# Another order for the second attention stage of a three-stage transformer kernel

## The reference

```python
def compress_blocks(a, pe, w1, w2):          # keys or values in overlapping blocks of 32
    ...
    blocks = blocks + pe[:, None, :]
    return jax.nn.gelu(flat @ w1) @ w2

def nsa_attend(q, gates, k_cmp, v_cmp, k_slc, v_slc, k_win, v_win):
    ...
    p_c = masked_softmax(s, ...)             # over the compressed blocks
    p_s = masked_softmax(s, dist_s >= 0)     # over the selected blocks: here all, as there are four
    p_w = masked_softmax(s, mask_w)          # over the window: here all earlier tokens
    return gi[..., 0:1] * o_c + gi[..., 1:2] * o_s + gi[..., 2:3] * o_w

def nsa_layer_mix(h, shared, mem_k, mem_v, w_in, w_out):
    q, gl, mq = split_cols(h @ w_in, [NSA_WIDTH, 3 * NSA_HEADS, MEM_WIDTH])
    gates = jax.nn.sigmoid(gl.reshape(B, T, NSA_HEADS, 3))
    o = nsa_attend(q * NSA_DH ** -0.5, gates, *shared)
    m = mem_attend(mq, mem_k, mem_v)         # four heads over 256 memory tokens
    return jnp.concatenate([o, m], axis=-1) @ w_out
```

## Time and profile before

| | |
|---|---|
| time of the runs shown | 1009.38 us, the median of 3 (1009.30 to 1010.58) |
| time of the profiled execution | 1014.77 us |
| its span, first to last instruction | 1013.5 us |
| mean granted clock of PE | 0.978 of 2.4 GHz |
| PE matmul, PE weight load | busy 968.8 and 940.7 us |
| DVE, ACT, POOL | busy 662.7, 504.5 and 25.3 us |

### The profile page before, as it was taken

The page is one execution under the profiler, slowest core; times in us unless marked ns, Lnnn a source line. Parts: engine busy times, 40 slices in busy tenths (PEclk is TensorE's granted clock), DMA queues, the critical chain, the costliest instruction groups (busy, mean ns, idle before and its releaser), DMA issues.

```text
span 1013.5 us, 18812 instructions
## 1 busy us (share of the span) xinstructions
PE 968.8 (96%) x7963; PEld 940.7 (93%) x7963; DVE 662.7 (65%) x1196; ACT 504.5 (50%) x837; POOL 25.3 (2%) x29
## 2 busy tenths in 40 slices
PE   6899999999999999887899999999999899999998
PEld 5899989999999998776899999999988799999998
DVE  5778856786767676664488676767455386556564
ACT  5544545554545473764456454546234364444442
POOL 0000000000000000000000000000022000000000
PEclk9999999999999989989999999999999899999999
DMA  9433333455454534331254645454321145454541
GB/s 353 164 146 125 125 125 114 178 196 219 152 219 152 222 137 136 125 126 42 74 218 177 229 167 208 167 209 156 136 92 63 55 161 213 168 207 167 208 167 42
DMA packets 24851, 160.66 MB, mean 159 GB/s; under 512 B 2880, under 2 KB 4672, under 8 KB 6080
## 3 DMA queue, kind: packets, MB, share of 16 engines
q1 hardware_dynamic: 24192, 159.20, 42.5%
q10 hardware_dynamic: 576, 0.26, 0.1%
HBM read 158.14 MB, written 1.05 MB: 157 GB/s over the span
## 4 chain that ended last, share of the span: by engine, by line
PE 87%; DVE 8%; ACT 3%; issue 1%; DMA 1%; SPq 0%; DVEq 0%; ACTq 0%
PE ps L358 86%; DVE wl L1134 3%; PE ps L367 1%; ACT wh L1889 1%; DMA raw<-in_w 1%; ACT arena L2121 1%; DVE arena L1566 1%; DVE xl L1143 0%; DVE col L1143 0%; DVE arena L1391 0%; DVE arena L1615 0%; DVE arena L1198 0%; SPq L2321 0%; DVE arena L1190 0%; DVE arena L1379 0%
## 5 line engine op out<-in xcount | busy, mean ns | idle before, releaser
L1134 DVE TENSOR_TENSOR wl<-raw,wh 128x1024 fp32r<-128x1024 f32 x292 | 342.0, 1220 | 156.3 <-ACT wh L1889 156.3
L358 PE MATMUL ps<-xh,wh 128*128 128x256 f32 (+1 forms) x1312 | 374.2, 285 | 10.7 <-DVE wl L1134 9.7
L358 PE MATMUL ps<-xl,wh 128*128 128x256 f32 (+1 forms) x1312 | 369.3, 282 | 0.0
L358 PE MATMUL ps<-xh,wl 128*128 128x256 f32 (+1 forms) x1312 | 368.9, 281 | 0.0
L1889 ACT CAST wh<-raw 128x1024 fp32r<-128x1024 f32 x292 | 290.2, 1046 | 155.9 <-PE ps L358 144.4
L358 PEld LDWEIGHTS ps<-xh,wh 128*128 128x128 f32 x1312 | 249.3, 190 | 14.2 <-DVE wl L1134 9.9
L358 PEld LDWEIGHTS ps<-xh,wl 128*128 128x128 f32 x1312 | 249.3, 190 | 0.0
L358 PEld LDWEIGHTS ps<-xl,wh 128*128 128x128 f32 x1312 | 249.3, 190 | 0.0
L358 PE MATMUL ps<-fh,wh 128*128 128x256 f32 x528 | 148.6, 282 | 0.0
L358 PE MATMUL ps<-fl,wh 128*128 128x256 f32 x528 | 148.6, 281 | 0.0
L358 PE MATMUL ps<-fh,wl 128*128 128x256 f32 x528 | 148.4, 281 | 0.0
(11 more groups left out here) (212 smaller groups left out, 1060.0 us busy)
## 6 DMA issues: line engine op xcount, KB each, us to landing
raw<-in_w SPq DMA_DIRECT2D x145, 1024.0 KB, 4.8
raw<-in_w SPq DMA_DIRECT2D x2, 512.0 KB, 6.0
arena<-in_mem SPq DMA_DIRECT2D x1, 1024.0 KB, 12.2
out<-xt SPq DMA_DIRECT2D x8, 128.0 KB, 2.0
small<-in_small SPq DMA_DIRECT2D x1, 943.5 KB, 9.0
arena<-in_sel SPq DMA_DIRECT2D x3, 256.0 KB, 5.5
xt<-in_x SPq DMA_DIRECT2D x2, 256.0 KB, 4.3
xt<-in_x SPq DMA_DIRECT2D x1, 512.0 KB, 6.3
```

The source lines that it names most:

```text
L358: return pe.matmul(out, lhsT, rhs, start=start, stop=stop, skip_group_check=True)
L1134: v.tensor_tensor(L[:, s], src[:, s], f32(H[:, s]), ALU.subtract).then_inc(*w_lo.up(2 * i + a))
```

## The change

The program computes the same, with these differences:

- Bq0 stands third in the list of units, in front of kvv; ck1 stands in front of Bq1.
- The squares of the tokens for stage B are taken at the end of f0, between the entries of chunks, and DVE adds them up to two (`square_sums("B")`), so that PE's sums are the short form that the other stages use (`sums`), placed between the halves of kvk. In all residuals the squares are taken later, and DVE's sums stand together at the start of the feed-forward stage.
- kvv comes after the gates are turned. The first score work of a pair, the compression halves, the halves of Bq1, Bm0 and Bm1 and the turns follow each other in another order; memory heads 0 and 1 run beside pairs 2 and 3.
- The gates' sigmoid is written as 1 / (1 + exp(−x)): ACT exponentiates, DVE adds 1 and takes the reciprocal.
- The four small transfers of the compression blocks go from ACT's queue to SP's, in front of the load of Bq1.
- Bo0, Bo1 and Bo2 are each ended before the next is (chunks 4 to 7 of each in one piece), and Co0 to Co2 of the last attention stage are ended in turn.
- Banks and the engines' lists follow.

```diff
-        + ["kvc", "kvk", "kvv", "Bq0", "ck0", "Bq1", "ck1", "cv0", "cv1", "Bm0", "Bm1",
+        + ["kvc", "kvk", "Bq0", "kvv", "ck0", "ck1", "Bq1", "cv0", "cv1", "Bm0", "Bm1",
...
         unit_f("kvc", 0, CH, CL, kv_in)
-        P = ps.open("sums_B", 4)
-        t.wait_ge(*ps.vacant("sums_B"))
-        for c in range(8):
-            t.wait_ge(*s_sq.at(SQ["B"] + c))
-            for n in range(2):
-                last = mm(P[:, n:n + 1], sqB[c][:, n * 128:(n + 1) * 128], cn("inv", 0, 1), c == 0 and n == 0, c == 7)
-        last.then_inc(*ps.full("sums_B"))
-        unit_f("kvk", 1, CH, CL, kv_in)
+        part_f("kvk", 1, range(0, 4), kv_in, CH, CL)
+        sums("B", 4)
+        part_f("kvk", 1, range(4, 8), kv_in, CH, CL)
         norm_spread("B", 5, rst_)
-        unit_t("kvv", lambda: 2, CH, CL, kv_in)
         unit_f("Bq0", 3, XH, XL, x_b)
         P = ps.open("gates", 0)
...
         nsa_scores(0)
-        squeeze(0, 0, 1)
-        P = ps.open("gates_t", 2)
+        P = ps.open("gates_t", 1)
         t.wait_ge(*ps.vacant("gates_t"))
         t.wait_ge(*ps.done("gates"))
...
-        part_f("Bq1", 0, range(0, 4), x_b)
+        unit_t("kvv", lambda: 2, CH, CL, kv_in)
         nsa_scores(1)
-        part_f("Bq1", 0, range(4, 8), x_b)
+        squeeze(0, 0, 0)
+        nsa_turn(0)
         squeeze(0, 1)
-        nsa_turn(0)
+        part_f("Bq1", 1, range(0, 4), x_b)
+        nsa_out(0)
+        nsa_turn(1)
+        part_f("Bq1", 1, range(4, 8), x_b)
+        nsa_out(1)
         squeeze(1, 0, 2)
-        nsa_out(0)
+        nsa_scores(2)
         squeeze(1, 1)
-        nsa_turn(1)
-        part_f("Bm0", 0, range(0, 4), x_b)
-        P = ps.open("gT", 1)
+        nsa_scores(3)
+        part_f("Bm0", 1, range(0, 4), x_b)
+        P = ps.open("gT", 0)
...
-        nsa_out(1)
-        nsa_scores(2)
-        part_f("Bm0", 0, range(4, 8), x_b)
+        nsa_turn(2)
         P = ps.open("kvm", 2)
...
-        nsa_scores(3)
+        part_f("Bm0", 1, range(4, 8), x_b)
+        blocks_scores(0, (7, 0))
+        blocks_scores(1, None)
+        nsa_out(2)
+        mem_scores(1, 0, 4, mqB, qB)
         part_f("Bm1", 1, range(0, 4), x_b)
-        blocks_scores(2, 0)
-        nsa_turn(2)
+        nsa_turn(3)
+        mem_scores(1, 1, 0, mqB, qB)
+        blocks_turn(7)
         part_f("Bm1", 1, range(4, 8), x_b)
-        mem_scores(1, 0, 0, mqB, qB)
-        nsa_out(2)
-        blocks_turn(7)
-        nsa_turn(3)
-        mem_scores(1, 1, 1, mqB, qB)
-        mem_turn(1, 0, 0)
+        mem_turn(1, 0, 4)
         nsa_out(3)
         blocks_out()
+        mem_out(1, 0, 5)
         mem_scores(1, 2, 7, mqB, qB)
-        mem_out(1, 0, 1)
-        mem_turn(1, 1, 0)
-        out_part("Bo0", lambda: 4, (0, 1), out_b, 0, 7)
-        mem_scores(1, 3, 7, mqB, qB)
-        out_part("Bo1", lambda: 5, (0, 1), out_b, 0, 7)
...
+        mem_turn(1, 1, 4)
+        mem_scores(1, 3, 0, mqB, qB)
+        out_part("Bo0", lambda: 6, (0, 1), out_b, 0, 7)
+        mem_out(1, 1, 7)
+        mem_turn(1, 2, 4)
+        out_part("Bo1", lambda: 1, (0, 1), out_b, 0, 7)
+        mem_out(1, 2, 5)
+        mem_turn(1, 3, 4)
         out_part("Bo0", None, (2, 3), out_b, 0, 7)
-        mem_out(1, 3, 1)
         out_part("Bo1", None, (2, 3), out_b, 0, 7)
+        mem_out(1, 3, 7)
+        out_part("Bo2", lambda: 2, (0, 1), out_b, 0, 7)
         out_part("Bo2", None, (2, 3), out_b, 0, 7)
         for j in range(3):
-            out_part(f"Bo{j}", None, (4, 5), out_b, 0, 7)
-        for j in range(3):
-            out_part(f"Bo{j}", None, (6, 7), out_b, 0, 7)
-        out_part("Bo3", lambda: 7, KORD, out_b, 0, 7)
+            out_part(f"Bo{j}", None, range(4, 8), out_b, 0, 7)
+        out_part("Bo3", lambda: 3, KORD, out_b, 0, 7)
```

VectorE's list, cut to the first half of the stage:

```diff
+        square_sums("B")
         rests("kvc", 2)
         token_variance("B")
...
         queries(0)
+        rests("Bq0", 2)
         d.wait_ge(*d_even.at(3))
...
-        rests("Bq0", 2)
+        d.wait_ge(*ps.ready("gates"))
+        v.tensor_copy(gz, ps["gates"][0:24, 0:T]).then_inc(*ps.freed("gates"))
+        nsa_scores(0)
+        d.wait_ge(*ps.done("gates_t"))
+        v.tensor_scalar(gt, gt, 1.0, None, ALU.add).then_inc(*n_ge.up(1))
+        d.wait_ge(*n_ge.at(1))
+        v.reciprocal(gt, gt).then_inc(*n_ge.up(2))
...
+        rests("kvv", 2)
+        nsa_probs(0)
+        nsa_scores(1)
...
         rests("ck0", 2)
-        nsa_probs(0)
+        nsa_probs(1)
+        rests("ck1", 2)
         rests("Bq1", 2)
-        nsa_scores(1)
         queries(1)
-        rests("ck1", 2)
-        nsa_probs(1)
         rests("cv0", 2)
+        nsa_scores(2)
+        nsa_probs(2)
+        nsa_scores(3)
+        take("gT", gT, 120)
         rests("cv1", 2)
...
+        add_up("Bo0", 0, "f1")
         rests("Bo0", 3)
-        add_up("Bo0", 0, "f1")
+        split_two(0, "f1", "gffn1")
+        residual("Bo1", 1, "f1", "gffn1")
         rests("Bo1", 3)
```

ScalarE's list, and the transfers on SyncE's:

```diff
+            for c in ((), (0, 1), (2, 3), (4, 5, 6, 7))[q]:
+                squares("B", c, xs[c])
...
-        a.wait_ge(*n_evn.at(0))
-        for g in range(2):
-            for par in range(2):
-                s.dma_start(X25[par * 64:(par + 1) * 64, :, g, :], ev5[g * 64:(g + 1) * 64, :, par, :]).then_inc(
-                    *d_even.up(2 * g + par))
...
+        for n in range(2):
+            last = s.activation(gt[:, n * 24:n * 24 + 24], ps["gates_t"][:, n * 24:n * 24 + 24], ACT.Exp,
+                                scale=nrst[:, 1 - n:2 - n])
+        last.then_inc(*ps.freed("gates_t"))
         nsa_exps(0)
...
         casts("ck0", 2)
+        nsa_exps(1)
+        nsa_turned(0)
+        casts("ck1", 2)
         casts("Bq1", 2)
...
+        nsa_turned(1)
+        casts("cv0", 2)
+        nsa_exps(2)
         gelu(0)
...
+            if NAMES[i] == "Bq1":
+                q.wait_ge(*n_evn.at(0))
+                for g in range(2):
+                    for par in range(2):
+                        load(X25[par * 64:(par + 1) * 64, :, g, :], ev5[g * 64:(g + 1) * 64, :, par, :], d_even, 2 * g + par)
```

The last attention stage, on PE:

```diff
-        for j in range(3):
-            out_part(f"Co{j}", None, (0, 1), out_c)
-        for j in range(3):
-            out_part(f"Co{j}", None, (2, 3), out_c)
+        out_part("Co0", None, (0, 1), out_c)
+        out_part("Co1", None, (0, 1), out_c)
+        out_part("Co0", None, (2, 3), out_c)
+        out_part("Co2", None, (0, 1), out_c)
+        out_part("Co1", None, (2, 3), out_c)
+        out_part("Co2", None, (2, 3), out_c)
```

More of the change, by code:

```diff
@@ L778, in nsa_out, with blocks_scores @@
             last.then_inc(*n_pv.up(j))
-        def blocks_scores(*on):
-            for g in range(2):
-                ps.open(f"cs{g}", on[g])
-                t.wait_ge(*ps.vacant(f"cs{g}"))
+        def blocks_scores(n, on):
+            if n == 0:
+                for g in range(2):
+                    ps.open(f"cs{g}", on[g])
+                    t.wait_ge(*ps.vacant(f"cs{g}"))
             t.wait_ge(*ps.done("kvm"))
             t.wait_ge(*ps.done("Bq1"))
-            for n in range(2):
[L788 to L794, removed]
+            for j in range(4):
+                for g in range(2):
+                    r = g * 64
+                    last = mm(ps[f"cs{g}"][:, n * 64 + j * 16:n * 64 + j * 16 + 15],
+                              bq[r:r + 64, j, (1 - n) * 128:(2 - n) * 128], kcm[r:r + 64, 0:15], True, True)
+                    if n == 1 and j == 3:
+                        last.then_inc(*ps.full(f"cs{g}"))
         def blocks_turn(bank):
@@ L813, in blocks_out, with part_f @@
                     last.then_inc(*ps.full(name))
-        def part_f(name, bank, chunks, ready):
+        def part_f(name, bank, chunks, ready, a_h=XH, a_l=XL):
             i = U[name]
@@ L1518, in dve_program @@
         by_rs("kvk", kk, rs_[:, 0:T])
[L1519 to L1524, removed]
+        v.tensor_scalar(nrst, rst_[:, 0:2], -1.0, None, ALU.mult).then_inc(*n_ge.up(0))
         def queries(n):
@@ L1622, in dve_program @@
                             ALU.subtract).then_inc(*n_rl.up(kv))
-        d.wait_ge(*ps.ready("gates"))
-        v.tensor_copy(gz, ps["gates"][0:24, 0:T]).then_inc(*ps.freed("gates"))
-        nsa_scores(0)
-        g0 = gt[:, 24:48].rearrange("p (h n) -> p h n", n=3)[:, :, 0]
-        d.wait_ge(*ps.done("gates_t"))
-        v.tensor_scalar(g0, g0, cn("valid", 0, 1), None, ALU.mult).then_inc(*n_gt.up(0))
+        rests("kvv", 2)
+        nsa_probs(0)
+        nsa_scores(1)
+        d.wait_ge(*ps.ready("kvv.0"))
+        for i in range(2):
+            last = v.tensor_scalar(vv[:, i * 256:(i + 1) * 256], ps["kvv.0"][:, i * 256:(i + 1) * 256],
+                                   rst_[:, i:i + 1], None, ALU.mult)
+        last.then_inc(*ps.freed("kvv.0"))
         rests("ck0", 2)
-        nsa_probs(0)
+        nsa_probs(1)
+        rests("ck1", 2)
         rests("Bq1", 2)
-        nsa_scores(1)
         queries(1)
-        rests("ck1", 2)
-        nsa_probs(1)
         rests("cv0", 2)
+        nsa_scores(2)
```

(25 more changed lines are left out.)

84 lines of the change are left out of this document (33 added, 51 removed).

## The result

The changed kernel takes **979.87 us** (976.86 to 980.68, four runs) where the kernel before takes 1009.41 (1009.30 to 1010.58, four runs): ratio 0.9699, 95% interval 0.9678 to 0.9721. The forecast was 980, with 976 to 989 as its range. The profiled executions are 1014.77 and 980.05 us, spans 1013.5 and 978.7, mean granted clocks 0.978 and 0.991.

A forecast was written before the change was run, and what follows sets the result against it. The prediction took TensorE, 96% busy, as the bound, losing time to latency waits and low clock behind them. Terms −3.8 −1.8 −16.7 −5.7 −0.5 −0.7 summed to −29.2, from 1009.38 to 980 us, range 976 to 989.

The forecast's parts named there:

- Waits: From kvc to f1u0, of TensorE's 18.56 us of standing still only 1.9 stay: −16.7 us.
- Sums: Stage B's 32 sums instructions become 8, −3.8 us; the slow-clock window behind them goes, −1.8 us.
- Clock: Four slow-clock windows behind TensorE's waits in the stage go: −5.7 us, bounds 5.0 and 6.3.
- Tails: Output units ended in turn remove the waits at f1u1, −0.5 us, and at Co3, −0.7 us.
- Gates: Gates by exponential save ScalarE table loads, but these lie beside TensorE work: no term of their own.
- transfers: The four block moves on SyncE's queue land just before VectorE wants them: cost nothing, cover 5.8 us.
- held-back squares: Later squares lengthen the chain ahead of the f0, f1 and f2 sums from 0.75 to 2.6 us, costing nothing.
- the saving is the same in both: Assumed the profiled execution, 1014.77 us, and the median run, 1009.38 us, both save 29.2 us.
- A: The clock falls behind the wait at the gates, perhaps also at nsa_turn(0): 985 us, chance 0.25.
- B: Several small margins in the stage fail together and half of the waits and slow clock returns: 991 us, chance 0.13.
- C: The stage's waits only move; just the sums, their slow window and output tails save: 1002.6 us, chance 0.04.
- D: The clock stays down through mixed small groups from the gates to the last memory turn: 1035 us, chance 0.03.

The follow-up runs named there:

- e7: Changed kernel with VectorE's copy of the gates moved ahead of the compression blocks; 980.58 us, ratio 0.9705.
- e1: Kernel before with only the short sums amid kvk and the squares at the end of f0; 1005.84 us, ratio 0.9952.
- e2: Changed kernel with the old 32 sums between kvc and kvk again; 984.60 us, ratio 0.9739.
- e3: Kernel before with output units of both attention stages ended in turn, squares held back and casts and low halves moved to match; 1007.08 us, ratio 0.9963.
- e4: Changed kernel with the gates by sigmoid on ScalarE again, without VectorE's addition and reciprocal; 977.76 us, ratio 0.9676.
- e11: Changed kernel with the four block moves back on ScalarE's queue, behind ck0's cast; 979.00 us, ratio 0.9687.
- e6: Changed kernel with VectorE's copy of the gates moved behind ck1's low halves; 983.88 us, ratio 0.9744.
- e8: Changed kernel with the gates' copy ahead of the compression blocks and ck1's low halves behind VectorE's second scores; 977.94 us, ratio 0.9675.
- e5: Changed kernel with kvv directly behind Bq0 on TensorE, ahead of the gates; 982.25 us, ratio 0.9730.
- e9: Changed kernel with the last attention stage's turn halves ahead of a weight's cast and low halves on ScalarE and VectorE; 974.80 us, ratio 0.9642.

## Why the prediction was right

**Waits, −16.7: right.** 18.56 to 1.74, −16.8. The schedule said 1.6 us at gates_t, and 1.46 was there; the steps came some 1 us earlier than written, on both engines alike (PE at gates_t at 386.8 for 387.7, the copy's end at 388.2 for 389.3), 0.8 of it because kvc itself starts at 364.0 for 364.8. nsa_turn(0), for which 0.3 was left, came out even, and mem_out(1,2), which had 0.25 to spare, waits 0.2. That DVE has no pause from 383 to 400 is the chain above, and e7 bears it out: relieved at one place, PE waits at the next.

**Sums, −3.8 and −1.8: right to within 1 or 2 us.** 4.75 us became 0.95, and the slow window behind them went. Stage e1 says 6.4, stage e2 5.8, the times 4.0 to 4.8, for a term of 5.6.

**Clock, −5.7: right in kind, undersized by some 2.** The stage's busy time fell by 13.4, the terms for sums, their slow window and clock add up to 11.3. The term was taken 0.6 under its bound of 6.3, and one of the four windows was cut too narrow: behind 484:488 the clock is still 0.88, another 0.5 us. The stage's row has more, (1 − 0.92) × 143.3 = 11.5 us of missing clock against 8.6 in the five windows of the earlier trace rows (4.7 × 0.48, and the 6.3 of the bound), but it also counts low clock under the sums themselves (0.74 from 370.7 to 375.3) and in waits, where PE does nothing with it. Of before, a window in a wait and the one behind 484:488:

```profile
447.20:450.80 3.60, 0.06 (x2) 0.00 (x0) 3.25 (x13) 2.79 (x13) 0.00 (x0) 0.62 0.52 221
```

```profile
488.00:492.00 4.00, 4.00 (x28) 3.89 (x28) 0.84 (x2) 0.96 (x2) 0.00 (x0) 0.88 0.30 127
```

A bound between the two was to be had; some 1 us of the 2 stays open.

**Tails, −1.2: undersized.** Both waits went, but e3 gives 3.0 by medians and 3.7 by the ratio, and behind the stage after saves 3.8. A part is lower loss to the clock between the profiled executions; why it was lower, and the rest, stay open.

**Gates 0, transfers 0, held-back squares 0: right** for the first two by e4 and e11. The squares were not run by themselves; e3 holds them, and is faster.

**The step that failed: "the saving is the same in both".** The terms were summed on the profiled execution of before, 1014.77, and the sum of 29.2 was then taken from the median. Between the profiled executions the saving is 34.7, between the medians 29.5. The forecast for the profiled execution, 985.6, was 5.5 too high: the clock (2.1) and what lies behind the stage (2.6) were too small, and kvc started 0.8 earlier. On the median it came right by luck, because two errors cancelled: the terms were too small for the execution they were read from, and that execution lost more to the clock than the median one. The 23 runs of before beside e1 to e4 show the spread: the eleven with a mean clock of 0.983 took 1007.7 to 1010.6 us, the eight with 0.979 or less 1011.4 to 1015.6. The profiled one, at 0.978, was of the second sort. The 0.005 of clock between it and the first sort are 0.005 × 1013 = 5 us of missing clock, about the 5.4 by which it lies above the median.

**Rivals.** A (985) did not come: the clock behind gates_t is 1.00. e6 made it, with 983.9. B and C are out by the 1.7 us of waits. D, the clock down through the mixed groups, is out: 332 matmuls, the pairs' small groups and halves of units in turn, from 394.5 to 430 at 1.00. So the section "A second HAM failure mode: psum-queue depth-cycling" of the Trainium skill's page "TensorE: Matmul & The Clock Gate", named in the prediction, did not decide here: the clock did not swing. But with 0.06 us of pause in 35.5 PE hardly idled between groups, and so this stretch does not test the case of that section, a PE that does. Nearer to it is a window of before, in which PE stood still between its groups for 2.26 of 10 us, and that is at 1.00 too:

```profile
455.00:465.00 10.00, 7.74 (x59) 6.02 (x59) 5.39 (x13) 4.29 (x12) 0.00 (x0) 1.00 0.00 0
```

## What to carry to other kernels

Write out each engine's list with the durations of its rows before moving a step: the waits that remain were found here to within half a us, and the largest belongs to the engine whose list has no pause (here DVE), so that moving one item only moves the wait (e7) and taking work out of the list removes it (e8). Price the clock by windows that go on until it is back at 1.00, and count it only where PE is busy: windows cut short gave too little here, the whole stage's row too much. Before summing terms on a profiled execution, compare its clock with that of the plain runs: if it is lower, the median has less to give back.

## What the runs showed of the hardware

**The same wait does not always cost the clock.** The turn in the last attention stage waits 2.92 us, for the same instruction, in before, after, e1 to e8 and e11. The windows of 4 us behind it have the clock at 1.00 in e1, e4, e5 and e7 and at 0.50 to 0.66 in the other seven; in after, e7 and e5 in this order (busy times, then the clock):

```profile
764.60:768.60 4.00, 3.96 (x21) 3.97 (x22) 0.00 (x0) 0.36 (x1) 0.00 (x0) 0.57 0.61 242
```

```profile
764.80:768.80 4.00, 3.95 (x33) 3.95 (x34) 0.00 (x0) 0.36 (x1) 0.00 (x0) 1.00 0.59 246
```

```profile
768.30:772.30 4.00, 3.97 (x33) 3.97 (x34) 0.00 (x0) 0.36 (x1) 0.00 (x0) 1.00 0.62 246
```

The same work, 21 matmuls in one and 33 in the others: 12 × 0.12 = 1.4 us. And the 1.55 us in e7, with the 0.24 behind them, brought 0.57, where 1.46 in after and 1.85 in before brought nothing. The prediction's line between 1.85 and 2.3 us was thus a coincidence of one trace. What decides was not found. Executions of one kernel differ in clock as well, as after's 976.86 at 0.995 and 979.68 to 980.68 at 0.991 show; one profile of each kernel does not tell at which places.

**The clock also falls behind small matmuls without a wait.** The 32 sums show it in before and e2, and eight sums in their place left it at 1.00 (e1, after). Behind 24 two-column sums and three transposes that PE runs without a pause, after has

```profile
709.00:714.00 5.00, 5.00 (x30) 5.00 (x31) 2.29 (x8) 4.12 (x6) 4.92 (x2) 0.66 0.00 0
```

and in it 14 matmuls from 710.38 to 713.37, one each 0.214 us, where the 17 from 703.94 to 705.95 took 0.118 each: 1.8 times, the factor that the prediction took for rival D. Another such place is not stable: behind 16 matmuls with eight rows, after has 0.58 in the first window below and e9 1.00 in the second; e4, whose order there is after's, also has 1.00 from 730 to 734:

```profile
730.00:734.00 4.00, 4.00 (x23) 3.75 (x21) 0.24 (x1) 0.00 (x0) 0.64 (x1) 0.58 0.00 0
```

```profile
728.00:732.00 4.00, 4.00 (x31) 3.49 (x31) 1.52 (x4) 0.00 (x0) 0.64 (x1) 1.00 0.31 129
```

**A table load delays by its own length only.** In after the load for the exponential stands in front of the gates on ACT:

```profile
388.51 1.28 ACT L2144 ACT_TABLE_LOAD   x1
389.81 0.45 ACT L2144 ACTIVATE arena<-ps,arena 128x24 f32<-128x24 f32 x2
```

The first exponential starts 0.02 us behind it. The Trainium skill, "ScalarE: Activation LUTs", section "What ACT_TABLE_LOAD costs", gives 1.28 us for the load, which agrees, and 1.38 more for a drain, which these rows don't show.
